# A feed-forward layer's sums in another order: chunk 1's weight sums, two raw products, and the last chunk's buffer

## The reference

```python
gate, up = jnp.split(jnp.einsum('bsd,df->bsf', hn, w_gate_up[l]), 2, axis=-1)
h = h + jnp.einsum('bsf,fd->bsd', jax.nn.silu(gate) * up, w_down[l])
return rms_norm_2(h, final_norm_w)      # D_MODEL 1024, D_FF 2816
```

## Time and profile before

| | |
|---|---|
| median of three runs | 807.11 us |
| the profiled execution | 810.11 us |
| its span, first to last instruction | 808.2 us |
| TensorE busy | 760.6 us, 94% |
| VectorE busy | 346.9 us, 43% |
| ScalarE busy | 190.1 us, 24% |
| mean granted clock of TensorE | 0.985 |

### The profile page before, as it was taken

The page is one execution under the profiler, slowest core; times in us unless marked ns, Lnnn a source line. Parts: engine busy times, 40 slices in busy tenths (PEclk is TensorE's granted clock), DMA queues, the critical chain, the costliest instruction groups (busy, mean ns, idle before and its releaser), DMA issues.

```text
span 808.2 us, 9616 instructions
## 1 busy us (share of the span) xinstructions
PE 760.6 (94%) x3873; PEld 503.8 (62%) x3873; DVE 346.9 (43%) x734; ACT 190.1 (24%) x418; POOL 56.0 (7%) x56
## 2 busy tenths in 40 slices
PE   5799999899999999999989999999989999999986
PEld 3478778677434343433334885888878888884432
DVE  1136424654622121212121866255456565568235
ACT  5122333542411110111011346122212111111002
POOL 2142553000000000000001000000000000000000
PEclk9899999999999999999999999998999999999999
DMA  9977895635959999999999943311435636435101
GB/s 355 392 219 248 323 356 179 222 140 218 380 195 416 414 420 411 418 415 414 419 406 363 374 158 105 105 41 65 127 123 168 197 121 202 166 146 192 68 27 55
DMA packets 76632, 197.25 MB, mean 244 GB/s; under 512 B 3263, under 2 KB 37416, under 8 KB 70184
## 3 DMA queue, kind: packets, MB, share of 16 engines
q1 hardware_dynamic: 75632, 195.37, 64.4%
q10 hardware_dynamic: 664, 0.80, 0.3%
q0 software_dynamic: 288, 0.41, 0.2%
HBM read 195.33 MB, written 1.05 MB: 243 GB/s over the span
## 4 chain that ended last, share of the span: by engine, by line
PE 77%; SPq 8%; DVE 7%; DMA 5%; ACT 2%; issue 1%; DVEq 0%; ACTq 0%
PE ps L1451 16%; PE ps L1173 9%; PE ps L740 8%; PE ps L1512 8%; PE ps L863 6%; PE ps L1247 4%; SPq L556 4%; PE ps L1087 4%; DMA ring<-in_w_in 3%; DMA arena<-in_w_up 2%; SPq L562 2%; PE ps L872 2%; PE ps L1049 2%; PE ps L1256 2%; PE ps L1059 2%; PE ps L1157 2%
## 5 line engine op out<-in xcount | busy, mean ns | idle before, releaser
L1173 PE MATMUL ps<-ring,arena 128*64 128x512 f32 x352 | 77.5, 593 | 2.0 <-DMA ring<-in_w_up 1.8
L863 PE MATMUL ps<-hs,ring 128*128 128x256 f32 (+1 forms) x288 | 67.8, 391 | 1.9 <-DMA ring<-in_w_in 1.9
L863 PEld LDWEIGHTS ps<-hs,ring 128*128 128x128 f32 (+1 forms) x288 | 53.5, 190 | 13.8 <-issue 6.5
L1173 PEld LDWEIGHTS ps<-ring,arena 128*64 128x64 f32 x352 | 25.9, 137 | 52.2 <-issue 51.9
L2746 DVE SCALAR_TENSOR_TENSOR arena<-arena,own_rows,ps 128x256 f32<-128x256 f32 x16 | 7.7, 480 | 111.0 <-ACT arena L1833 111.0
L740 PE MATMUL ps<-hs,ring 128*128 128x256 f32 x240 | 53.1, 380 | 0.3 <-PE ps L740 0.3
L740 PEld LDWEIGHTS ps<-hs,ring 128*128 128x128 f32 x240 | 45.3, 190 | 6.9 <-issue 0.7
L1451 PE MATMUL ps<-arena,mixT 128*128 128x256 f32 x176 | 42.5, 385 | 3.5 <-DVE mixT L2632 3.5
L1451 PE MATMUL ps<-ring,mixT 128*128 128x256 f32 x176 | 42.6, 385 | 0.0
L1451 PE MATMUL ps<-ring,hs 128*128 128x256 f32 x176 | 41.7, 379 | 0.9 <-DVE xT L2620 0.9
L1247 PE MATMUL ps<-ring,arena 128*64 128x512 f32 x176 | 40.2, 598 | 1.1 <-issue 0.5
(11 more groups left out here) (468 smaller groups left out, 1238.9 us busy)
## 6 DMA issues: line engine op xcount, KB each, us to landing
ring<-in_w_down SPq DMA_DIRECT2D x23, 1024.0 KB, 19.1
ring<-in_w_gate_up SPq DMA_DIRECT2D x22, 1024.0 KB, 7.5
ring<-in_w_gate SPq DMA_DIRECT2D x20, 1024.0 KB, 16.3
ring<-in_w_up SPq DMA_DIRECT2D x20, 1024.0 KB, 17.5
ring<-in_w_ada SPq DMA_DIRECT2D x5, 3072.0 KB, 14.2
ring<-in_w_down SPq DMA_DIRECT2D x5, 2048.0 KB, 8.0
ring<-in_w_in SPq DMA_DIRECT2D x9, 1024.0 KB, 18.2
ring<-in_w_ada SPq DMA_DIRECT2D x16, 512.0 KB, 11.7
```

Of the source, the lines that this page charges most:

```text
L863: last = pe.matmul(o[0:n, 0:L], lhsT=w[:, k, lo:lo + n], rhs=hT[:, k, :], start=k == 0, stop=k == KT - 1)
L1173: last = pe.matmul(ps[WIN * h:WIN * (h + 1), 0, :].rearrange("p (g n) -> p g n", g=2), lhsT=xw[:, u, k, :], rhs=expert_gate_up(2 * n + h, ...
```

## The change

Three edits. The weight sums of gate/up chunk 1 (`ffn_sum(1)`) are made after "u" of chunk 0, where the later chunks have theirs, and no longer ahead of the token sums. The products 11 and 12 of down chunk 1 are done right after those of chunk 0, ahead of the wait for chunk 0's weight sums. The weight sums of the last down chunk go to columns 1408 to 1919 of `hT`, `mixT` and `sq`, and VectorE no longer waits for chunk 3 to be used before it makes them.

```diff
+        def down_sums(c):
+            if c == DOWN_N - 1:
+                return [t[:, (FT // 2) * P:(FT // 2) * P + 512] for t in
+                        (hT.rearrange("p k t -> p (k t)"), mixT[:].rearrange("p k t -> p (k t)"), sqf)]
+            return [ffn_sums[:, (FFN_N + c) % 2, i].rearrange("p k n -> p (k n)") for i in range(3)]
...
                 down_part("12", 0)
+                chunk_there("down", 1)
+                down_part("11", 1)
+                down_part("12", 1)
                 sums_there(0)
                 down_part("4", 0)
...
                     for name in DOWN_PARTS:
+                        if c == 1 and name in ("11", "12"):
+                            continue
                         last = down_part(name, c)
...
-                    if n > FFN_N + 1:
+                    if FFN_N + 1 < n < FFN_N + DOWN_N - 1:
                         ve.wait_ge(chunk_used, NUMBER["down", n - FFN_N - 2] + 1)
...
-                ffn_sum(1)
                 ve.wait_ge(scaled, SCALED[4] + KT)
...
                     ve.tensor_tensor(u, q, acc[3], ALU.add).then_inc(parts_ready, 1)
-                    if 0 < n < FFN_N - 1:
+                    if n < FFN_N - 1:
                         ffn_sum(n + 1)
-                    elif n:
+                    else:
                         down_sum(0)
```

More of the change, by code:

```diff
@@ L1501, in down_part @@
                     w = weights("down", c, min(DOWN_STEP, FT - c * DOWN_STEP), D)
-                    sums = ffn_sums[:, (FFN_N + c) % 2].rearrange("p i k n -> p i (k n)")
+                    sums = down_sums(c)
                     for i in range(min(DOWN_STEP, FT - c * DOWN_STEP) // 2):
@@ L1506, in down_part @@
                                      "12": (h_pair[:, n, 1, 0:P], w[:, 2 * i + 1, 0:512]),
-                                     "4": (h_pair[:, n, 1, P:L], sums[:, 2, col]),
-                                     "5": (h_sums[0][:, n, :], sums[:, 0, col]),
-                                     "6": (h_sums[1][:, n, :], sums[:, 1, col]),
+                                     "4": (h_pair[:, n, 1, P:L], sums[2][:, col]),
+                                     "5": (h_sums[0][:, n, :], sums[0][:, col]),
+                                     "6": (h_sums[1][:, n, :], sums[1][:, col]),
                                      "7": (h_sums[2][:, n, :], w[:, 2 * i, 512:D]),
@@ L2600, in down_sum @@
                     w = weights("down", c, k, D).rearrange("p (n j) d -> p n j d", j=2)
-                    sums = ffn_sums[:, n % 2].rearrange("p i k n -> p i (k n)").rearrange("p i (n d) -> p i n d", d=512)
+                    sums = [t.rearrange("p (n d) -> p n d", d=512) for t in down_sums(c)]
                     ve.wait_ge(arrived[SLOT["down", c]], ARRIVED["down", c])
                     weight_sum(n, *(w[:, :, j, at:at + 512] for j in range(2) for at in (0, 512)),
-                               [sums[:, i, 0:k // 2] for i in range(3)])
+                               [t[:, 0:k // 2] for t in sums])
                 def h_sum(n, done):
```

## The result

| | before | after |
|---|---|---|
| first comparison, median of four runs each | 807.08 us (806.79 to 810.26) | 799.7 us (798.47 to 800.72) |
| ratio, with its 95% interval | | 0.9883 (0.9852 to 0.9914) |
| second comparison, medians of 24 and 6 runs | 809.51 us (805.91 to 812.18) | 798.22 us (795.49 to 799.15) |
| ratio | | 0.9866 (0.9838 to 0.9894) |
| profiled execution | 810.11 us, span 808.2 | 798.86 us, span 797.0 |

The change makes the kernel 1.2 or 1.3% faster by the two ratios. (A ratio is not the quotient of the two medians beside it, which is 0.9909 in the first comparison, inside the interval, and 0.9861 in the second.) I forecast 795.7 us (a ratio of 0.986). The first comparison's 799.7 is 4.0 us more and lies 0.2 us inside the upper end of the range, 799.9. In the traces the feed-forward became 11.2 us shorter, against 11.4 forecast.

What follows compares the result with a forecast made beforehand. The prediction took TensorE, busy 94% of the span, as the bound, with time to win only where it is idle or slow. Gains of 5.1 + 1.3 + 5.0 = 11.4 us from the 807.11 median gave 795.7 us, range 794.0 to 799.9.

Steps and rivals of the forecast that it cites:

- Part A: Gate/up chunk 0, chunk 1's weight sums behind token sums: 3.6 wait plus 1.8 clock minus 0.3 new wait, 5.1 us.
- new wait: TensorE ahead of gate/up chunk 1 waits for gate 1 of chunk 0: about 0.3 us, bounds 0 and 1.5.
- table load: ScalarE's silu table load in chunk 0, 1.28 us, said to be over ahead of gate 1; cost taken as 0.
- Part B: Products 11 and 12 of down chunk 1 ahead: stretch from turn to "7" 3.46 to 2.15 us, 1.3 gained.
- Part C: Last down chunk: chunk 5's sums in their own place, without the wait: 3.2 wait plus 1.8 clock, 5.0 us.
- Rival 1: Low clock stays once or twice in the feed-forward: 1.8 or 3.6 us less gain, 797.5 or 799.3 us; chance 0.12.
- Rivals 2 to 4: VectorE late in chunk 0, 799.9 us (0.04); chunk 5's load last, 800.7 (0.03); down chunk 1's load late, 815.5 (0.01).
- rival 2: Gate/up chunk 0: moved sums hold up gate 1 by 2.4 us, low clock 1.8 more; 799.9 us, chance 0.04.

Runs made afterwards that it cites:

- kernels with the place alone: Kernel before plus chunk 5's sums in their own place, wait for chunk 3 kept, traced twice: feed-forward 222.6 and 224.3 us.
- filled waits: Kernel before plus three unused products in the wait for chunk 5's sums (ratio 0.998), or in chunk 0's token-sum wait too (ratio 0.997).
- early start: Changed kernel with gate 1 of chunk 0 ahead of chunk 1's sums and first product waiting for only four residual tiles: median 799.5 us, ratio 0.9878.
- first-edit kernel: Kernel before with only chunk 1's weight sums moved behind the token sums: ratio 0.9939, feed-forward 220.6 us.

## Why the prediction was right, and where it was off

**Part A, 5.1 us forecast.** 601.95 - 596.75 = 5.2 measured up to chunk 1. The token sums began at 584.48 (584.5 forecast) and TensorE's next part at 587.46 (587.47). Gate 1 began at 596.19, not 596.38: in the steady chunk whose row I used the operation also had to wait for product "4", which ends there at 611.03 + 1.89 = 612.92, and in chunk 0 that product is long done. (This reason fits the rows; no run tests it.) The new wait is 0.2 us, not 0.3. The gated products ended at 598.50 against a turn at 600.28, a cover of 1.8 us; I had given 0.7. Most of the difference is that the 3.0 us I took from the steady chunk hold 0.90 us in which VectorE waits there for a product, at 614.68, and chunk 0 has no such wait. The table load was not over ahead of gate 1 as I said: it ran from 595.10 to 596.38, into gate 1. It cost nothing, as the silu behind it started at 597.05 and waited for the reciprocal.

**Part B, 1.3 us forecast.** 732.82 - 730.67 = 2.15 us from turn to "7", as forecast, before 3.46. Chunk 2's sums ended at 743.47 and chunk 2 began at 747.43: 4.0 us of cover, 4 forecast.

**Part C, 5.0 us forecast.** Product to product 772.34 - 770.63 = 1.71 us, and two final products in 777.49 - 772.34 = 5.15. Chunk 5's sums ended at 767.5, 4.9 us ahead of their use, 4 forecast. The kernels with the place alone show that the gain came from leaving out the wait, and none from the place.

**The low clock.** That at these two waits the idle time brings it is shown by the filled waits: full clock at the end in three traces of three, where an empty wait of 3.0 us gave it in one of six, and in chunk 0 in one of one, where the empty wait gave it in none of nine. It does not follow that idle time is the only thing that brings it: the second mixer had it in nine traces with TensorE busy almost throughout. Its size, which I took as fixed at 1.8 us each, is fixed only behind the wait of chunk 0 (nine traces). Behind the one at the end it was 0 to 3.0 us, with a mean of 1.65 over six traces, so the sum stays near 11.2 as a mean and is not a property of each execution. Rival 1, that the low clock stays, did not happen in either trace of the changed kernel, nor in that of the early start. Rivals 2 to 4 each need a wait of TensorE in the feed-forward, and the changed kernel's traces list none but the 0.9 us for the residual (the 0.2 us for gate 1 shows in the start times). In these traces the length of a slow stretch times what its mean granted clock lacks of 1.00 comes near the loss by the start times: 0.33 x 5.25 = 1.7 us and 0.25 x 6.92 = 1.7 us with the earlier trace rows, against 1.8 each, and over 774.64 to 782.81 of the first-edit kernel 0.36 x 8.17 = 2.9 us, against 3.0.

**The step that was off** is the last, "From the median: 807.11 - 11.4". The three runs behind that median lay low: 24 runs later gave a median of 809.51 and 26 more 808.53. The other part of the miss is in the changed kernel's own four runs, 798.5, 798.9, 800.6 and 800.7, whose median is 1.5 us above the later 798.22. Against 795.7 that makes 2.4 us of base and 1.6 us above the forecast from the later base. So it was in part luck that 799.7 fell inside the range: its upper end came from rival 2, which did not happen. The traces put most of the spread, 6 to 9 us among runs of the kernel before, ahead of the feed-forward: its first product starts between 578.24 and 588.43 us, though no kernel but the one with the early start changes anything ahead of it. This also makes my last sign, that I am wrong if the stretch ahead changes by a microsecond or more, a bad one: it moved by 4.5 us with no edit. I saw that the profiled execution was 3.0 us above the median, called it without effect on the gain, which is right, and then took the lower number as the base, and set the lower end of the range by the spread of the three runs. Scaled to the second comparison's 809.51 the forecast sum gives 798.1, where 798.22 was measured. Smaller slips changed nothing: the chances of the forecast and rivals 1 to 3 add up to 0.97, not the 0.96 given for faster, and 743.5 + 4.84 is 748.3, not 748.6.

**Additivity.** The three edits alone gave 3.7, 1.5 and 4.9 us in their traces, 10.1 in sum; with the end's low clock at the 1.8 us of the trace before in each, 4.9, 1.3 and 4.9, which is 11.1 of the 11.2.

## What to carry to other kernels

When TensorE is the bound, list its waits in a stage, and price each with the slow products behind it: the sum of start times up to the first product of normal length, not the idle time alone. Take that price from several traces: behind one wait it was 0 in one and 3.0 us in another. An operation whose consumer is far off, queued ahead of one whose consumer is waiting, was the cheapest thing to move here; then work out which consumer is next. And take the base of a forecast from as many runs as the kernel's spread asks for: stages that a change does not touch can move the time by more than the change, and a stage's own length, from trace to trace, was good to 0.2 us here where the low clock was the same.

## What the runs showed of the hardware

- Behind 2.2 us of idle TensorE the granted clock fell to 0.50 of full speed in one trace of one, behind 2.3 us in ten of fourteen, behind 3.0 us in five of six, behind 3.5 us in nine of nine. In the kernel before, behind chunk 0's wait of 3.5 us, it was 0.50 from 592.1 to 595.1 us and 1.00 again from 596.1. In the feed-forward it stayed at 1.00 behind 0.9 us (thirteen traces) and 1.0 us (ten).
- It also fell, in nine traces of fourteen, in a stretch of the second mixer in which TensorE was busy for 14.85 to 15.00 of 15 us (mean granted clock 0.77).
- The same program behind the same 3.0 us wait lost 0 us in one execution and 1.8 in another; over all kernels with that wait it was 0, 1.5, 1.8 or 3.0 us.
- Useless products in a wait gave 1.7 us back at each of two places: two parts in 3.56 us, not 5.25, and two final products in 5.23, not 6.92.
- Writing sums to `hT`, `mixT` and `sq` took 0.69 us per 128x512, and in the arena 0.68 or 0.69.
